# The last projection of a two-block network on one core: output tiles 2 to 15 in pairs of seven block products

## What is computed

```python
def second_block(x, c, norm_g, w_ada, b_ada, w_in, ...):
    ...
    mod = c_act @ w_ada[l] + b_ada[l]
    shift, scale, gate = jnp.split(mod, 3, axis=-1)
    ...
    y = jnp.concatenate([att, hg], axis=-1) @ w_out[l]
    x = x + gate[:, None, :] * y
```

## Time and profile before

| | |
|---|---|
| runs, median | 1868.37 us |
| span of the profiled execution | 1866.6 us |
| PE busy | 1860.7 us, 100% of the span |
| DVE busy | 1207.5 us, 65% |
| ACT busy | 797.6 us, 43% |
| POOL busy | 188.2 us, 10% |
| share of PE in the chain that ended last | 98% |

### The profile page before, as it was taken

How to read it: one execution, slowest core, us unless ns; L and a number is a source line. 1 busy time by engine, 2 the same in 40 slices (tenths; PEclk the granted TensorE clock), 3 DMA queues, 4 the chain that set the end, 5 groups by cost and what they waited for, 6 DMA issues and landing times.

```text
span 1866.6 us, 25573 instructions
## 1 busy us (share of the span) xinstructions
PE 1860.7 (100%) x8710; PEld 1542.2 (83%) x8710; DVE 1207.5 (65%) x1753; ACT 797.6 (43%) x1177; POOL 188.2 (10%) x185
## 2 busy tenths in 40 slices
PE   9999999999999999999999999999999999999999
PEld 8888888888888877887888888888888888888887
DVE  6665678888888877677754444445656666666332
ACT  6543433333333373323644444444554555554111
POOL 3500000000000002443000000000222222210000
PEclk9999999999999999999999999999999999999999
DMA  7344145544454436666122222222221222123431
GB/s 284 113 158 180 67 161 177 180 167 162 166 178 162 155 113 221 239 230 218 72 94 70 90 93 93 84 79 90 83 76 71 86 90 90 67 91 136 152 140 67
DMA packets 50551, 244.70 MB, mean 131 GB/s; under 512 B 5704, under 2 KB 7240, under 8 KB 29904
## 3 DMA queue, kind: packets, MB, share of 16 engines
q1 hardware_dynamic: 50064, 241.02, 36.3%
q10 hardware_dynamic: 448, 3.17, 0.4%
HBM read 235.75 MB, written 8.41 MB: 131 GB/s over the span
## 4 chain that ended last, share of the span: by engine, by line
PE 98%; DVE 1%; ACT 0%; issue 0%; DVEq 0%; ACTq 0%
PE ps_p L633 28%; PE ps_p L635 28%; PE ps_p L634 28%; PE ps_o L798 1%; PE ps_s L994 1%; PE ps_t L782 1%; PE ps_x L652 1%; DVE act_lo L2068 1%; PE ps_s L771 0%; PE ps_s L770 0%; PE ps_s L772 0%; PE ps_o L658 0%; DVE wk L2063 0%; PE ps_o L1031 0%; PE ps_t L736 0%; PE ps_t L735 0%
## 5 line engine op out<-in xcount | busy, mean ns | idle before, releaser
L633 PE MATMUL ps_p<-act_hi,w_hi 128*128 128x512 f32 x2272 | 905.7, 399 | 0.3 <-DVE w_lo L1569 0.3
L635 PE MATMUL ps_p<-act_hi,w_lo 128*128 128x512 f32 x2272 | 886.2, 390 | 0.0
L634 PE MATMUL ps_p<-act_lo,w_hi 128*128 128x512 f32 x2272 | 885.8, 390 | 0.0
L635 PEld LDWEIGHTS ps_p<-act_hi,w_lo 128*128 128x128 f32 x2272 | 426.5, 188 | 90.9
L633 PEld LDWEIGHTS ps_p<-act_hi,w_hi 128*128 128x128 f32 x2272 | 427.1, 188 | 83.0 <-issue 1.2
L634 PEld LDWEIGHTS ps_p<-act_lo,w_hi 128*128 128x128 f32 x2272 | 427.4, 188 | 80.2 <-issue 0.7
L1079 ACT ACTIVATE w_hi<-raw 128x2048 fp32r<-128x2048 f32 x153 | 292.5, 1912 | 387.0 <-PE ps_p L635 368.4
L1564 DVE TENSOR_TENSOR w_lo<-raw,w_hi 128x2048 fp32r<-128x2048 f32 x151 | 346.2, 2293 | 85.6 <-ACT w_hi L1079 73.9
L1859 DVE CUSTOM_DVE_ANT_0 mkv<-mkv,c_all 128x1024 f32<-128x1024 f32 x96 | 145.7, 1553 | 3.6 <-DVE wk L1606 2.9
L2375 POOL TENSOR_TENSOR ssq_a<-ssq_a,wk 128x512 f32<-128x512 f32 x15 | 36.3, 2419 | 725.0 <-ACT wk L1343 725.0
L2395 POOL TENSOR_TENSOR hz<-hqk,hd 128x128 f32<-128x128 f32 x48 | 34.8, 725 | 726.6 <-DVEq L2233 688.7
(11 more groups left out here) (379 smaller groups left out, 1930.2 us busy)
## 6 DMA issues: line engine op xcount, KB each, us to landing
raw<-wt_dram SPq DMA_DIRECT2D x156, 1024.0 KB, 4.8
mkv<-ada_dram SPq DMA_DIRECT2D x96, 512.0 KB, 4.3
qkv<-xT_dram SPq DMA_DIRECT2D x16, 256.0 KB, 2.8
spill_dram<-Y SPq DMA_DIRECT2D x16, 256.0 KB, 2.2
hqk<-spill_dram SPq DMA_DIRECT2D x16, 256.0 KB, 2.7
out_dram<-wk SPq DMA_DIRECT2D x15, 256.0 KB, 2.0
Y<-xT_dram SPq DMA_DIRECT2D x3, 1024.0 KB, 10.0
mem_raw<-memT_dram SPq DMA_DIRECT2D x4, 512.0 KB, 11.0
```

The source lines that it names most:

```text
L633: mm(o, wh, hi[:, k, 0:n], start=at == 0, stop=False)
L634: mm(o, wh, lo[:, k, 0:n], start=False, stop=False)
L635: last = mm(o, wl, hi[:, k, 0:n], start=False, stop=at == KT - 1)
```

## The change

`out2` now has 2 tiles in the old form. The other 14 are 7 pairs in the new phase `fast`. For a pair (two output tiles, f = 0 and 1) the weights are four blocks of 128 x 1024, (f, k) with k the lower or upper half of the input channels; the activations are four blocks of 1024 channels x 256 tokens. The 2 x 2 product of blocks is made by Winograd's form of Strassen's scheme: seven products instead of eight, of sums and differences of blocks.

- **Activations, once.** VectorE overwrites `Y` in eight steps of 128x4x256 with the four sums (`token_sums`); ScalarE rounds them into `t_hi` (`token_high`, eight copies of 128x1024), VectorE takes the rest into `y_lows`, which lies where `Y` lies (`token_low`, eight of 128x1024). It begins when all 16 slices of `act_hi` and `act_lo` are made.
- **Weights, per pair.** VectorE makes four sums of 128x1024 (`first_sums`, `last_sums`) in the memory of `mkv`; ScalarE makes seven `w_hi` blocks (`block_high`), VectorE seven `w_lo` blocks (`block_low`), 128x1024 each. Four slots hold the blocks.
- **Products.** Each is 8 slices of `k` x 3 matmuls of 256 columns, 24 in all, into one of three accumulators (`product`). A product waits for its block's split and for the reading of its bank.
- **Results, per pair.** VectorE reads the accumulators six times at 128x256 (`read_bank`), ScalarE copies one twice with the gate applied (`copy_corner`), GpSimd adds it to or subtracts it from the scaled rows of `x` three times at 128x256. VectorE scales the two rows of `x` beforehand (`scale_x`, 128x512 each).
- SyncE loads weights in halves of 512 KB. Rows of `x` go to `x_even` or to `wk[:, 2:4]`.

The diff, cut to its core:

```diff
@@ PHASES
-    "out2": (8, 2),
+    "out2": (1, 2),
+    "fast": (7, 2),
@@ tensor
+            def product(p, n):
+                pe.wait_ge(block_split.sem, block_split.at("fast", p, (1, 2, 3, 5, 6, 7, 4)[n]))
+                hi, lo, split_tokens = token_blocks[n]
+                if p == 0 and split_tokens:
+                    pe.wait_ge(token_split, split_tokens)
+                if n == 0 and p >= 2:
+                    pe.wait_ge(bank_read.sem, bank_read.at("fast", p - 2, 6))
+                elif 1 <= n <= 2 and p:
+                    pe.wait_ge(bank_read.sem, bank_read.at("fast", p - 1, 3 + n))
+                elif n == 4:
+                    pe.wait_ge(corner_copied.sem, corner_copied.at("fast", p, 1))
+                elif n >= 3:
+                    pe.wait_ge(bank_read.sem, bank_read.at("fast", p, (1, None, 2, 3)[n - 3]))
...
+                for k in range(HALF_K):
+                    c = slice(k * P, (k + 1) * P)
+                    mm(o, wh[:, c], hi[:, k, :], start=n < 3 and k == 0, stop=False, skip_group_check=True)
+                    mm(o, wh[:, c], lo[:, k, :], start=False, stop=False, skip_group_check=True)
+                    last = mm(o, wl[:, c], hi[:, k, :], start=False, stop=k == HALF_K - 1, skip_group_check=True)
+                last.then_inc(product_done.sem, 1)
@@ scalar
+            out2(0)
+            for n, c in TOKEN_ORDER:
+                token_high(n, c)
...
+            for p in range(NFAST):
+                for n in (0, 1, 2, 6, 3):
+                    block_high(p, n)
+                copy_corner(p)
+                block_high(p, 4)
+                block_high(p, 5)
@@ vector
-            loop(dve, "out2", out2, peel=1, head=1, order=o)
+            dve.wait_ge(moving_hi, 1 + 4 * KT)
+            dve.wait_ge(moving, 1 + 4 * KT)
+            do(ts(less_gate[:, :], mod[:, 2 * KT:3 * KT], -1.0, None, ALU.mult))
+            for n, c in TOKEN_ORDER[0:2]:
+                token_sums(n, c)
+            for n, c in TOKEN_ORDER[2:8]:
+                token_sums(n, c)
+            for c in range(2):
+                token_low(2, c)
+            for c in range(2):
+                token_low(0, c)
...
+            first_sums(0, 0)
+            first_sums(0, 1)
+            block_low(0, 0)
+            for c in range(2):
+                token_low(1, c)
+            block_low(0, 1)
+            block_low(0, 2)
+            for p in range(NFAST):
+                if p:
+                    read_bank(p - 1, 5)
+                block_low(p, 6)
+                last_sums(p, 2)
+                scale_x(p)
+                read_bank(p, 0)
+                block_low(p, 3)
+                last_sums(p, 3)
+                block_low(p, 4)
+                read_bank(p, 1)
+                block_low(p, 5)
+                if p == 0:
+                    out2(PLAIN - 1, 1)
+                    for c in range(2):
+                        token_low(3, c)
+                read_bank(p, 2)
+                if p < NFAST - 1:
+                    first_sums(p + 1, 0)
+                    first_sums(p + 1, 1)
+                    block_low(p + 1, 0)
+                    if p == 0:
+                        out2(PLAIN - 1, 0)
+                    block_low(p + 1, 1)
+                read_bank(p, 3)
+                read_bank(p, 4)
+                if p < NFAST - 1:
+                    block_low(p + 1, 2)
+            read_bank(NFAST - 1, 5)
@@ gpsimd
+            for p in range(NFAST):
...
+                tt(x[:, 1, LATE_TOKENS], x[:, 1, LATE_TOKENS], corner[:, 1, :], ALU.subtract).then_inc(corner_added.sem, 1)
+                tt(x[:, 1, EARLY_TOKENS], x[:, 1, EARLY_TOKENS], corner[:, 1, :], ALU.subtract).then_inc(
...
+                tt(x[:, 0, LATE_TOKENS], x[:, 0, LATE_TOKENS], corner[:, 0, :], ALU.add).then_inc(corner_added.sem, 1)
```

More of the change, by code:

```diff
@@ L101 @@
 CONSTS = 2 * P
+PLAIN, NFAST = PHASES["out2"][0], PHASES["fast"][0]
+BLOCK = D // 2
+TOKENS = S // 2
+FAST_SLOT = (0, 1, 2, 0, 1, 2, 3)
 class Count:
@@ L174, in build @@
         gall = sb("gall", [P, KT])
+        less_gate = sb("less_gate", [P, KT])
         hcol = sb("hcol", [P, 8, NHG])
@@ L178, in build @@
         stat = sb("stat", [P, 6, QT])
+        with ExitStack() as early:
+            x_even = sb("x_even", [P, 2, S], F32, early)
         with ExitStack() as early:
@@ L431, in build, with fast_slot_free @@
         p2_lows = [p2_lo[:, c:c + S - j * P] for j, c in enumerate(CAUSAL_T)]
+        TOKEN_ORDER = [(n, c) for n in range(4) for c in range(2)]
+        def fast_slot_free(eng, p, n):
+            if 3 <= n < 6:
+                eng.wait_ge(product_done.sem, product_done.at("fast", p, n - 2))
+            elif p:
+                eng.wait_ge(product_done.sem, product_done.at("fast", p - 1, 7 if n == 6 else n + 4))
+            else:
+                eng.wait_ge(proj_done, tile_no("out2", PLAIN - 1, 0 if n < 2 else 1) + 2)
         def token_half(h):
@@ L507, in load @@
                 t = tile_no(phase, i, j)
-                if isinstance(t, int) and t + ahead >= NTILES:
+                if isinstance(t, int) and t + ahead >= TILE0["fast"] + 2:
                     return
@@ L605, in _ @@
+            sp.wait_ge(bank_read.sem, bank_read.at("fast", NFAST - 1, 6))
+            sp.dma_start(out[15][:, EARLY_TOKENS], wk[:, 1, EARLY_TOKENS]).then_inc(s_store[1], 16)
             for j in range(2):
@@ L1058, in out2 @@
             def out2(i):
-                first = isinstance(i, int)
+                first = isinstance(i, int) and i == 0
                 project("out2", i, 0, use="y2", hooks={3: last_sum} if first else None)
@@ L1073, in split @@
                 t = tile_no(phase, i, j) + ahead
-                if isinstance(t, int) and t >= NTILES:
+                if isinstance(t, int) and t >= TILE0["fast"]:
                     return
@@ L2330, in _, with token_sums @@
-            loop(dve, "out2", out2, peel=1, head=1, order=o)
+            def token_sums(n, c):
+                k, t = token_parts(n, c)
+                if n in (0, 1):
+                    other = (token_parts(1, c), token_parts(2, c))[n]
+                    op = ALU.subtract
+                elif n == 2:
+                    dve.wait_ge(token_sum, 3 + c)
+                    other, op = token_parts(0, c), ALU.add
+                else:
+                    dve.wait_ge(token_sum, 5 + c)
+                    other, op = token_parts(2, c), ALU.subtract
+                tt(Y[:, k, t], Y[:, k, t], Y[:, other[0], other[1]], op).then_inc(token_sum, 1)
@@ new lines, in _, with first_sums @@
+            dve.wait_ge(moving_hi, 1 + 4 * KT)
[9 more added lines that the diff above has]
+                token_low(0, c)
+            def first_sums(p, n):
+                if n == 0:
+                    if p:
+                        dve.wait_ge(s_block[2], 16 * p)
+                        dve.wait_ge(s_block[3], 16 * p)
+                        dve.wait_ge(block_split.sem, block_split.at("fast", p - 1, 5))
+                    else:
+                        for f in range(2):
+                            dve.wait_ge(s_raw[slot("fast", f)], 16 * (half("fast", 0, f) + 1))
+                    tt(block_sums[0], raw_block(1, 0), raw_block(1, 1), ALU.add).then_inc(block_sum.sem, 1)
+                else:
+                    if p:
+                        dve.wait_ge(s_block[0], 16 * p)
+                        dve.wait_ge(block_split.sem, block_split.at("fast", p - 1, 7))
+                    dve.wait_ge(block_sum.sem, block_sum.at("fast", p, 1))
+                    tt(block_sums[1], block_sums[0], raw_block(0, 0), ALU.add).then_inc(block_sum.sem, 1)
@@ new lines, in last_sums @@
+            def last_sums(p, n):
+                if n == 2:
+                    dve.wait_ge(block_split.sem, block_split.at("fast", p, 3))
+                    tt(block_sums[0], raw_block(0, 0), raw_block(1, 0), ALU.add).then_inc(block_sum.sem, 1)
+                else:
+                    if p:
+                        dve.wait_ge(s_block[1], 16 * p)
+                    dve.wait_ge(block_split.sem, block_split.at("fast", p, 1))
+                    tt(block_sums[1], block_sums[1], raw_block(0, 1), ALU.add).then_inc(block_sum.sem, 1)
@@ new lines, in block_low, with scale_x @@
+            def block_low(p, n):
+                dve.wait_ge(block_hi.sem, block_hi.at("fast", p, (1, 2, 3, 5, 6, 7, 4)[n]))
+                tt(fast_slot(n, w_lo), FAST_FROM[n], fast_slot(n, w_hi).bitcast(F32), ALU.subtract).then_inc(
+                    block_split.sem, 1)
+            def scale_x(p):
+                i = p + PLAIN
+                dve.wait_ge(s_stage[i % 2], 16 * 8 + 32 * (i // 2) + 32)
+                for j in range(2):
+                    x = x_rows[i % 2][:, j, :]
+                    stt(x, x, col("final_g", 2 * i + j), r1[:, :], ALU.mult, ALU.mult).then_inc(x_scaled, 1)
```

200 lines of the change are left out of this document (164 added, 36 removed).

## The result

The changed kernel takes 1873.35 us (median of 9 runs, 1873.25 to 1873.53), the kernel before 1868.37 (9 runs, 1868.04 to 1868.93). The ratio is 1.0026, with a 95% interval of 1.0018 to 1.0034: slower by 5.0 us, just above the 0.2% (3.7 us) that the prediction takes as what a measurement can tell. The profiled execution has a span of 1871.7 us, 5.1 more than before.

The account below looks back on a forecast made before the run. TensorE's work was taken as the bound (busy 1860.7 of 1866.6 us). Terms: -11.3 matmuls, +9.1 first wait, +5.2 catching up, 0 clock, -0.4 end = +2.6, so 1868.37 becomes 1871.0 us; range 1865.0 to 1876.5.

Parts of the forecast that it names:

- likeliest case: Whole kernel: the summed forecast of 1871.0 us with its own range, 1868.2 to 1874.4 us; chance 0.50.
- slower: Whole kernel: a time above 1872.1 us, beyond the 0.2% that counts as the same; chance 0.37.
- Matmuls: TensorE in out2: 672 wide matmuls (152.4 us) give way to 1176 of 256 columns (141.1 us), gaining 11.3 us.
- the rival with faster matmuls: Products: 256-column matmuls 0.107 us apart, not 0.120 as in memk; VectorE then limits pairs; 1862 us, chance 0.10.
- The first wait: Behind tile 1: TensorE idle 9.1 us (8.5 to 11) until VectorE's chain has the first product ready at 1719.8.
- Catching up: First to eleventh product: VectorE's 34.0 us list is behind TensorE, 5.2 us of waits (3.0 to 6.7).
- The clock: First product after the idle gap: slow start loses up to 2.5 us, covered by TensorE's waits for VectorE; cost 0.
- The rival in which the slow clock outlasts the cover: Behind the gap: slow pace for three products, 7 us or more lost, 5 covered; 1873 to 1875 us, chance 0.05.
- its sign: Behind the gap: granted clock down for more than 5 us would show that the slow clock outlasts its cover.
- VectorE the bound: Last five pairs: GpSimd's work blocks VectorE, 21.2 us a pair against TensorE's 20.16; 1876 us, chance 0.18.
- The end: Program's close: one reading of 256 columns and one store instead of two half readings and two stores, -0.4 us.

Follow-up runs that it names:

- noshift: The changed kernel with the small tensor less_gate moved behind all tensors that the phases up to hg use: 1872.33 us, ratio 1.0022.
- nopool: The changed kernel without GpSimd's 21 additions and subtractions, their semaphores still raised: 1872.20 us, ratio 1.002.
- fewlows: The changed kernel without four of VectorE's eight token_low instructions, two products reading the low parts of other sums: 1872.11 us, ratio 1.0018.
- warm: The changed kernel with 38 extra, never-read matmuls of 512 columns between tile 1 and the first product: 1873.33 us, ratio 1.0026.
- b_shift: The kernel before with an unused tensor of 64 bytes a partition added ahead of hcol: 1870.09 us, ratio 1.0009.

## Why the prediction was right, and where it was not

The time, 1873.35, lies in the range (1865.0 to 1876.5) and in the likeliest case's own (1868.2 to 1874.4). It lies 2.35 us above the forecast, just on the side "slower", to which I had given 0.37 against 0.53 for no change. The mechanism holds: cheaper matmuls, one long wait for VectorE's chain, shorter waits up to the eleventh product, and then TensorE's pace. That the total is so near owes something to errors of opposite sign: in the profiled execution the steps that were foreseen are off by -0.9, -0.2, +1.8 and -0.3 us, and 1.9 us come from something that no step had. With the tensors at their old addresses (noshift, 1872.33) the forecast is off by 1.3.

- **Matmuls.** Predicted -11.3 us. The narrow ones came at 0.1193 instead of 0.1200 us: 1176 x 0.1193 = 140.3, so -12.2. noshift shows that the 0.0007 belong to the shifted tensors; without the shift memk's pace holds exactly (0.1200). That the extra cost lies in each matmul and not in memk's operands is shown, and the rival with faster matmuls (0.107) falls. The rule of the Trainium skill (TensorE: Matmul & The Clock Gate, Back-to-back issue gap) would give an estimate of 0.109 us for 256 columns. The trace does not agree, it has 0.010 more. The same section gives its rule for an isolated gap, and says that in a stream of weight loads and matmuls both set the distance; the matmuls here are such a stream.
- **The first wait.** Predicted 9.1 us beyond the normal distance; it is 1721.61 - 1712.53 - 0.23 = 8.85. The steps of VectorE's chain have the lengths from the rows of before: without the 1.9 us of shift the first product starts at 1719.7, predicted 1719.8. The 0.2 us less are tile 1, which took that much longer (its first two matmuls are 0.34 us apart).
- **Catching up.** Predicted 5.2 us, and this is the term of the sum that was mis-sized. From the first product to the last it is 144.4 us; 48 x 24 x 0.1193 would be 137.4, so 7.0 us were lost, of which the slow clock is 2.4 and waits the rest. The list from 1721.56 to the low part that frees the eleventh product (1757.05) took 35.5 us instead of 34.0. VectorE's timeline there has 1.4 us of waits for ScalarE (predicted 1.3), 0.7 for GpSimd and an instruction that took 1.22 us beside it instead of 0.75 (together 1.2; predicted up to 2.2, and nopool shows 1.15), 0.9 for a store and 0.3 for its own semaphore (both not in the sum), and 31.7 us of instructions instead of 30.5: where one waits for the one before, as at the evacuations, the overlap of 0.09 us is lost. So the list is 1.5 us longer than predicted, and ten products at 0.1193 take 0.2 less than 28.8. The store is missing from the prediction altogether: among the transfers priced at nothing it names the loads of weights and of `x`, and no store. One of TensorE's three waits, 1.26 us before (1,1), is for the reading (L2578) that this store held up. It also said that VectorE needs only the readings from the slow products; fewlows shows it waiting for ScalarE's copies, which waited for them.
- **The clock.** Predicted 0, with the loss covered: shown by warm. The rival in which the slow clock outlasts the cover did not happen, though its sign (a clock that is down for more than 5 us behind the gap) did by a little: the first product took 5.3 us, and from the second on the matmuls have the full pace.
- **VectorE the bound.** Did not happen. The predicted 17.4 to 19.6 us a pair have 1.3 us of waiting for ScalarE in them, so what compares with the busy 17.2 us is 16.1, the 80% that the prediction names; it is 86%. nopool has 16.8, so GpSimd's three operations, 4.85 us a pair, cost VectorE 0.4 us and not 2.2: nearly all of its work fits into the gaps.
- **The end.** Predicted -0.4: from the start of the last matmul to the end it was 3.7 us (span 1866.6) and is 2.9 (the last starts at 1868.76), so -0.7.
- **What no step had.** +1.9 us up to tile 1. "The order is unchanged up to here, so the time is too" was assumed without being said. b_shift gives the same 1.9 us in the runs' medians with no instruction added. In the profiled executions it is 1.9 in the changed kernel and 1.1 in b_shift, whose profiled run is one of its fastest (1869.63, median 1870.09). The start of tile 1 scatters from trace to trace: in the seven with the tensors where they were or 256 bytes further it lies at 1699.82 to 1700.77, in the seven with 64 bytes at 1700.90 to 1701.96. So the shift is there in all of them, and its size up to tile 1 is known to about 1 us only.

The sum by measured terms: -12.2 + 8.9 + 7.0 - 0.7 = +3.0 and +0.2 of rounding and of tile 1, then +1.9: 5.1, the difference of the spans.

## What to carry to other kernels

A change that makes fewer operations out of more preparation pays only if the preparation has a place: here seven pairs could save 12 us, and 16 us went into one wait at the border and the catching up behind it. Where the same preparation ran beside two more old-form tiles, with a pair less to gain from, the time fell by 7.3 us. When you take work off a late engine and little comes off the time, look at what that engine waits for next. Here it was a store that frees its target, moved by the order in the engine's own list, and loads queued behind such a store, moved by the order in a DMA queue. And put a new small tensor behind the ones in use, so that a measurement of the change is not one of its addresses.

## What the runs showed of the hardware that was not expected

- The position of tensors in SBUF changes the spacing of matmuls, both ways at once: with 64 bytes ahead, 256-column matmuls come 0.1178 us apart in memk and 0.1193 in the products instead of 0.1200, while the phases up to tile 1 take 1.1 to 1.9 us longer in single traces. With 256 bytes ahead it is as before. Which of the moved tensors does it is not known.
- The clock's fall and return are plain here: 0.96 on average in the first 4.4 us of the idle time, 0.50 for the 8 us from 1717 to 1725, of which TensorE worked in the last 3.4, and 1.00 from 1727 on; 38 filler matmuls kept it at 1.00. Behind the second one, the slow matmuls of 256 columns were 0.2135 us apart ((1726.90 - 1721.99) / 23), not 0.239 (twice the fast 0.1193). That is twice the 0.1069 that the prediction worked out for the columns alone, so of the 0.013 us on top of each matmul nothing is to be seen at the slow clock.
